# The long matmul of every weight tile in two halves, in a float32 network of two layers on one Trainium2 core

## What is computed

```python
def rms_norm(x, g):
    xf = x.astype(jnp.float32)
    y = xf * lax.rsqrt(jnp.mean(xf * xf, axis=-1, keepdims=True) + NORM_EPS)
    return (y * g.astype(jnp.float32)).astype(x.dtype)
...
m = jax.nn.silu(cond) @ w + b                       # 2048 x 12288, per layer
qkv = (h @ w_qkv)                                   # 2048 x 6144
op = attention(q, k, v) @ na_wo                     # 2048 x 2048
proj = h @ w_in                                     # 2048 x 10368
y @ w_out                                           # 4096 x 2048
xp = xp + mp[5] * (jnp.square(jax.nn.relu(hp @ mlp_w1[i])) @ mlp_w2[i])   # 2048 x 8192, 8192 x 2048
```

## Time and profile before

| | |
|---|---|
| median of 3 runs | 3342.05 us (3341.59 to 3345.84) |
| the profiled execution: its span, from first to last instruction | 3336.6 us |
| TensorE matmuls busy | 3119.8 us (94%), 17,357 instructions |
| TensorE weight loads busy | 2663.5 us (80%), 17,357 instructions |
| VectorE busy | 2215.8 us (66%) |
| ScalarE busy | 1723.2 us (52%) |
| HBM traffic | 208 GB/s over the span |

### The profile page before, as it was taken

How to read it: one execution, slowest core, us unless ns; L and a number is a source line. 1 busy time by engine, 2 the same in 40 slices (tenths; PEclk the granted TensorE clock), 3 DMA queues, 4 the chain that set the end, 5 groups by cost and what they waited for, 6 DMA issues and landing times.

```text
span 3336.6 us, 47767 instructions
## 1 busy us (share of the span) xinstructions
PE 3119.8 (94%) x17357; PEld 2663.5 (80%) x17357; DVE 2215.8 (66%) x2980; ACT 1723.2 (52%) x2247; POOL 44.2 (1%) x71
## 2 busy tenths in 40 slices
PE   6899998989999999999699999966698999999998
PEld 4688887878888888888588888856587888888887
DVE  7866666777666676675666566777766665666565
ACT  5655555555455454454466555567443444444443
POOL 1000000000000000000000000011000000000000
PEclk9999999999999999999899999977899999999999
DMA  9777774757567576674477655556254555555552
GB/s 321 267 273 262 272 274 151 263 197 271 189 239 252 182 271 214 218 273 151 162 253 252 241 176 189 188 171 192 81 188 151 169 184 189 189 179 186 190 188 88
DMA packets 378477, 696.17 MB, mean 209 GB/s; under 512 B 12192, under 2 KB 55392, under 8 KB 377360
## 3 DMA queue, kind: packets, MB, share of 16 engines
q1 hardware_dynamic: 373568, 676.38, 59.3%
q0 software_dynamic: 4816, 18.69, 1.6%
HBM read 686.50 MB, written 8.52 MB: 208 GB/s over the span
## 4 chain that ended last, share of the span: by engine, by line
PE 39%; DVE 7%; issue 2%; ACT 2%; DMA 1%; SPq 1%; DVEq 0%; ACTq 0%; POOL 0%; POOLq 0%
PE bank L1111 24%; PE bank L1110 12%; PE bank L1094 1%; DMA bc_prompt<-ac_scratch 1%; DVE w_lo L697 1%; ACT w_hi L441 1%; PE bank L1113 1%; SPq L311 1%; DVE bc_prompt L992 0%; PE bank L1359 0%; DVE ROOM L746 0%; DVE xd L958 0%; DVE ROOM L751 0%; DVE ROOM L757 0%; DVE bc_prompt L948 0%
## 5 line engine op out<-in xcount | busy, mean ns | idle before, releaser
L697 DVE TENSOR_TENSOR w_lo<-raw,w_hi 128x1024 fp32r<-128x1024 f32 x1256 | 1481.1, 1217 | 731.3 <-ACT w_hi L441 730.9
L441 ACT ACTIVATE w_hi<-raw 128x1024 fp32r<-128x1024 f32 x1256 | 1268.0, 1050 | 1028.3 <-PE bank L1111 999.2
L1111 PE MATMUL bank<-HL,w_hi 128*128 128x512 f32 x4368 | 1549.7, 401 | 68.8 <-DVE HL L815 28.6
L1110 PE MATMUL bank<-HL,w_lo 128*128 128x256 f32 x4095 | 1162.8, 284 | 27.6 <-DVE HL L815 13.7
L1111 PEld LDWEIGHTS bank<-HL,w_hi 128*128 128x128 f32 x4368 | 814.4, 190 | 252.4 <-issue 61.3
L1111 PE MATMUL bank<-HID,w_hi 128*128 128x512 f32 x2560 | 894.2, 398 | 0.3 <-DVE w_lo L697 0.3
L1110 PEld LDWEIGHTS bank<-HL,w_lo 128*128 128x128 f32 x4095 | 781.1, 191 | 63.8 <-DVE w_lo L697 28.9
L1110 PE MATMUL bank<-HID,w_lo 128*128 128x256 f32 x2400 | 674.8, 281 | 0.0
L1111 PEld LDWEIGHTS bank<-HID,w_hi 128*128 128x128 f32 x2560 | 471.1, 188 | 105.1 <-issue 1.5
L1110 PEld LDWEIGHTS bank<-HID,w_lo 128*128 128x128 f32 x2400 | 453.6, 189 | 7.7 <-DVE w_lo L697 0.7
L787 DVE TENSOR_TENSOR U<-bank,U 128x256 f32<-128x256 f32 x433 | 181.1, 422 | 257.5 <-ACT U L490 257.4
(11 more groups left out here) (203 smaller groups left out, 1377.0 us busy)
## 6 DMA issues: line engine op xcount, KB each, us to landing
raw<-in_mlp_w SPq DMA_DIRECT2D x256, 1024.0 KB, 5.2
raw<-in_mod_w SPq DMA_DIRECT2D x192, 1024.0 KB, 6.0
raw<-in_ssm_w_in SPq DMA_DIRECT2D x80, 1024.0 KB, 5.0
raw<-in_na_wqkv SPq DMA_DIRECT2D x48, 1024.0 KB, 5.1
raw<-in_ssm_w_out SPq DMA_DIRECT2D x32, 1024.0 KB, 5.0
raw<-in_na_wo SPq DMA_DIRECT2D x16, 1024.0 KB, 5.0
bc_prompt<-ac_scratch SPq DMA_DIRECT2D x16, 512.0 KB, 5.7
bc_sample<-ac_scratch SPq DMA_DIRECT2D x16, 512.0 KB, 6.0
```

The source lines that it names most:

```text
L441: nc.scalar.activation(w_hi[:, T % 2, u * n:(u + 1) * n], raw[:, T % RAW_SLOTS, u * n:(u + 1) * n], ACT.Copy).then_inc(hi_ready, 1)
L697: nc.vector.tensor_tensor(w_lo[:, T % 2, s], raw[:, T % RAW_SLOTS, s], w_hi[:, T % 2, s], ALU.subtract).then_inc(lo_ready, 1)
L1110: nc.tensor.matmul(bank[b][:, 0:TOK], lo, a[:, 0:TOK], start=False, stop=False)
L1111: i = nc.tensor.matmul(bank[b][:, :], hi, a, start=first, stop=last)
```

## The change

The matmul with `w_hi` becomes two of 256 columns with the same weights, one into each half of the bank, and the one with `w_lo` comes behind both for every tile. The first matmul of a bank still carries `start`, the last one `stop`. Nothing else is altered.

```diff
                                 first, last = q == 0 and kt == 0, q == 3 and kt == 3
                                 a = A[:, 4 * q + kt, :]
-                                if not first:
-                                    nc.tensor.matmul(bank[b][:, 0:TOK], lo, a[:, 0:TOK], start=False, stop=False)
-                                i = nc.tensor.matmul(bank[b][:, :], hi, a, start=first, stop=last)
-                                if first:
-                                    i = nc.tensor.matmul(bank[b][:, 0:TOK], lo, a[:, 0:TOK], start=False, stop=False)
+                                nc.tensor.matmul(bank[b][:, 0:TOK], hi, a[:, 0:TOK], start=first, stop=False,
+                                                 skip_group_check=True)
+                                nc.tensor.matmul(bank[b][:, TOK:2 * TOK], hi, a[:, TOK:2 * TOK], start=False,
+                                                 stop=False, skip_group_check=True)
+                                i = nc.tensor.matmul(bank[b][:, 0:TOK], lo, a[:, 0:TOK], start=False, stop=last,
+                                                     skip_group_check=True)
                             return i
```

## The result

The changed kernel is slower: 3392.5 us in the median of 4 runs (3389.49 to 3398.46) against 3342.43 for the kernel before beside it (4 runs), a ratio of 1.0149 with a 95% interval of 1.0135 to 1.0164. Forecast were 3331 us, a gain of 11; the loss is 50.

A forecast was written before the change was run, and what follows sets the result against it. TensorE's matmul stream was taken to bound the kernel. Matmuls -11.8 us, loads and order nothing, the clock trimming it to -11, set against the median 3342.05 gave 3331 us, range 3300 to 3455.

The forecast's parts named there:

- The bound: Whole kernel: TensorE's matmuls, busy 3119.8 of 3336.6 us, set the time; ScalarE and VectorE run behind.
- the first part: Matmuls of all 6,928 weight tiles: three short slots replace a long and a short one, -11.8 us.
- 3 x 116.7: Changed weight tile: three 256-column slots, each start to start, at 116.7 ns make 350.0 ns.
- Today's tile: Weight tile before the change: 853 tiles begun in 300 us, taken as 351.7 ns per tile.
- the sum's -11.8: All weight tiles: -1.7 ns per tile times 6,928 gives -11.8 us, taken as -11 us after the clock.
- The modulation's 232.5: 512-column slots in the modulation: 232.5 ns against 213.3 for the columns, so something beyond the columns is paid.
- The weight loads: 6,928 added loads on TensorE: hidden under slots of 116.7 ns, as a load and matmul pair needs 111.7; cost nothing.
- The order: High, high, low replaces low, high in each tile: ScalarE's eviction some 0.1 us earlier at most, hidden.
- Rival 2: Weight tiles: each load takes stream time, 15.9 ns per matmul with load; 367.7 per tile, +111 us, 3453; chance 0.20.
- a pair 245: Argument against rival 2: two neighbouring short slots would then take 245 ns, where the trace shows 230.
- Rival 1: Weight tiles: a start cost per matmul, +3.4 ns per tile, +23.6 us, 3366; chance 0.10.
- Rivals 3 and 4: Weight tiles: half-slots of 117.5 ns, 3342, chance 0.10; loads alone setting 111.7 ns slots, -115 us, 3227, chance 0.15.

The follow-up runs named there:

- the kernel with turned runs: Kernel before with each bank's matmuls in runs of one size, every second bank taking the short ones first: 3335.53 us, ratio 0.9967.
- the sweep: Changed kernel with three matmuls per tile of other widths, 128 to 384 columns, in two kernels: slots from 110.6 ns (128) to 173.8 ns (384).
- the uneven split: Changed kernel with the `w_hi` matmul split into 288 and 224 columns instead of two of 256: 3413.84 us, ratio 1.0206 to the kernel before.

## Why the prediction was wrong

*The bound* was right: TensorE sets the time before and after the earlier trace rows, and the 7.0 ns per tile reached the end: 48.5 of 50 us. (The DMA engines' 0.57 in the earlier trace rows is a share, 57 of the 100 us, not 0.57 us; it leaves the bound as it is.)

*The step that failed* is in the first part, "So the short slot is about 116.7 ns wherever it stands, beside its like or beside a long one", and with it the term 3 x 116.7. The longest row of short slots of the rounded format in the trace of before is two, each with long ones around it. In a row without end a short slot is 120.0, and the kernel with turned runs shows both in one timeline: 0.23 us for two, 120 ns for each further one. Three of them are 360.0, 10.0 ns per tile over the 350.0. Today's tile was mis-sized too, 351.7 instead of 353.0, by the count that took in matmuls begun before the stretch. Together 8.7 ns per tile, 60 us: the way from the sum's -11.8 to the +48.5 of the slots. In the earlier trace rows a tile has 346.7 ns. I split it by the starts, 230 and 116.7; by the sweep's prices it is 227 and 120, the same sum. The starts in a mixed row stand some 3 ns off; the uneven split shows such shifts as well. The modulation's 232.5, which warned that the long slot too had more in it than its columns, I used for the rivals only.

*The weight loads* were costed rightly at nothing for their length: the floor is 111, as the earlier trace rows said, and three loads fit under three slots of 120. Whether a load as such costs nothing is not shown, since the 13 ns may be the matmul's or its load's. In the earlier trace rows the kernel has five norms, not ten: its 80 matmuls, on unrounded float32, stand in the trace as 160, each with a load, so that no load is left out, as the text says. The sixteen of the earlier trace rows are eight in the kernel, of unrounded float32 as well; the sweep has the same floor in the rounded format.

*The order* was costed rightly at nothing.

*Rival 2* had the form, a fixed price of a matmul with its load, and its test: three short slots over 117.2 ns. Its price of 15.9 was too high, since today's tile holds 6.3 ns of something else (353.0 - 346.7); hence 367.7 instead of 360.0, and 3453 instead of 3392. Its cause, that the load takes the time from the stream, is not borne out as far as its width goes: a narrower load changes nothing in proportion. Of the argument against it, "a pair 245, where the earlier trace rows show 230", the number was true and the conclusion wrong, for the reason above.

*Rival 1* had the sign and a price of 3.4, a quarter of the true one. The Trainium skill, "TensorE: Matmul & The Clock Gate", section "Back-to-back issue gap", gives N/2.4 + 2.5 ns, but calls it the gap of an isolated matmul, which the prediction left out. The sweep agrees with its form, an addend that does not grow with the columns. Its 2.5 ns differ from the 11 to 14 measured here, in the rounded format with a load for each matmul; the measurement decides.

*Rivals 3 and 4* were refuted: a half of a long slot is 120.0 and not 117.5, and nothing came near 335 per tile.

## What to carry to other kernels

A split of a matmul costs a fixed amount per added matmul (here 13 ns, 92 us for 6,928, of which some 40 came back because the mixed row of before was itself above its price), even where the added load is hidden; so use as few matmuls as the banks allow: two of 384 columns beat one of 512 and one of 256. Read the price of an instruction from whole periods of a steady row, or from a row of its like long enough to settle; in a mixed row the distance of two starts can lie 3 ns beside it, and 3 ns in each of three slots were more than the forecast's whole gain of 1.7. When matmuls are counted in a stretch, go from first start to last start; the plain count gave a tile 1 ns too little. When a forecast's gain is smaller than the step that it extrapolates (two in a row to an endless row), hold the other sign for just as likely.

## What the runs showed of the hardware

- In the rounded format a slot in a settled row is the columns at 2.4 GHz plus 11 to 14 ns, from 240 to 512 columns, and 110.6 to 111.7 ns from 128 to 224. At the lower clock level no such price is seen: 768 columns took 0.64 us in two matmuls, their time at 1.2 GHz.
- Loads of 112 and 100 weight columns instead of 128 left a 256-column slot at 117.9 and 120.0 ns.
- Where long and short matmuls alternate, two matmuls of together 768 columns took 346.7 ns in one chunk and 353.3 in another, and the order long, short, short, long 348.4 in a stretch in which the kernel before took 353.0.
- In one trace eight 256-column slots in a row between long ones took 0.95 us and two took 0.23, so 120 ns for each of the six more.
